# Memory projections of a hybrid encoder layer: whole fp32 matmuls in place of split fp32r ones, with earlier loads and a new order

## The chip, the cores and the metric

The kernel runs on one core of one Trainium2 chip. The metric is the device time of one launch in microseconds, taken over several runs; the time before is the median of three. The profile is of one further execution.

## The reference, cut to what matters

One layer of a streaming encoder over 1024 tokens of width 1024, in fp32:

```
h = rms_norm(x);  p = h @ w_in                      # 31 column tiles of 128 in the kernel
y = concat(rwkv7(p_a), conformer_conv(p_b), hgrn2(p_c), stick_breaking(p_d))
x = x + y @ w_out
h = rms_norm(x);  m = rms_norm(mem)                 # mem: 256 rows
q = h @ wq;  k = m @ wk;  v = m @ wv                # 4 heads of 256
o = softmax(q k^T / 16) v;  x = x + o @ wo;  out = rms_norm(x)
```

The four mixers are independent of each other until `w_out`. The memory `mem` depends on nothing before it. The kernel folds the products of weights with the memory: `keys = wq k^T` and `vals = v wo` for each head, so that the second sub-layer is `softmax(h @ keys) @ vals`.

## The kernel before, in words

**Split numbers.** TensorE takes fp32 in two ways here: an fp32 matmul, or an fp32r matmul on rounded numbers. For most products the kernel writes an operand as a rounded high part and a remainder and issues three fp32r matmuls (high by high, low by high, high by low). Weights are split by POOL (`whi` at line 855, `wlo` at line 856), activations by ACT (high) and DVE (low). The small products inside the mixers are fp32 matmuls of 64 by 64 (line 957, 1082, 1094 to 1097) and the block sums with 512 columns (979, 1110 to 1118).

**Stages.** (1) `xn`, `xT`: rows of x are normed and transposed into `act_hi`, `act_lo`. (2) The input projection, 31 tiles of `w_in`; each is 16 pieces (8 of k for each half of the tokens) of three matmuls with 512 columns (lines 911 to 913). (3) The mixers: a recurrent chain (`lora` to `rfin`, twice, then `hgate` to `hfin`, twice), a convolution chain on DVE, and a stick-breaking chain (`sbz`, `sbt`, `sbv`, 12 units for each pair of heads). In a unit, TensorE makes scores (1170) and, after ACT and DVE (a scan at line 1824), transposes (1183) and multiplies by v (1198); a unit waits for the unit before it. (4) The memory tiles: `mk` and `mv` (8 each, 8 pieces of three 256-column matmuls, lines 911 to 913), `qa` (8, 935 to 937, 256 columns, 8 pieces) and `vo` (8, 944 to 946, 512 columns, 4 pieces). `qa` and `vo` results go through six SBUF slots to DRAM (`keys_dram`, `vals_dram`, line 792). (5) `ysplit` (mixer output into `act_hi` by ACT at 1479, `act_lo` by DVE), then 12 "wide" products of 8 row tiles each, 24 matmuls with 256 columns per row tile (1222 to 1224): four with `w_out`, four with keys, four with values; POOL splits their weights too (842, 843).

**Order.** Stages 2 to 4 are interleaved. A planner in Python (`mixer_order`) simulates TensorE, ACT and DVE with fixed costs and picks at each step a chain's head or the next piece of a tile; its result is one list, and each engine's program follows that list in order. `TILE_RANK` orders the tiles, `URGENT` weighs delay of the four chains, `IDLE` weighs idle TensorE, `HOLD` delays two entries, `SUPPLY` is the time that a tile's weights take. Piece costs of the planner are 0.35 us for `mk`, `mv`, `qa` and 0.7 us for the others.

**Buffers and waits.** `mem_hi` to `v_lo`, `mem_raw` and `moved` lie where `act_hi` and `act_lo` lie, so the memory rows are loaded only after the last `w_in` tile (`load_mem`), and `mn` waits for them. Raw weights have two slots (`wraw`), and two more (`moved[2:4]`) for memory tiles. `x2`, `vhi`, `vlo0` lie over the mixers' buffer `A`, `vraw` at the end of `B` (the stick chain's). SP issues all loads and stores in one queue: after the last memory tile it stores, loads `w_out` parts into `vraw` once the stick chain's last output is read, and x into `x2` once all mixers are done. `ysplit` waits for all mixers and all stores.

Of the kernel before, what the change touches and what calls it, by code (L numbers as in the profile page):

```python
# [14 lines left out]
P = 128  # L15
# [14 lines left out]
KK_SCALE = 2.0 ** 16  # L30

# [9 lines left out]
for _n, _k in (("mu", 6), ("mux", 1), ("w0", 2), ("a0", 2), ("k_k", 2), ("k_a", 2), ("r_k", 2), ("rln_g", 2),  # L41
# [18 lines left out]
TILE_RANK = {t: n for n, t in enumerate((  # L60
# [6 lines left out]
HOLD = {('sv', 1): ('minit', 0, 1),  # L67
        ('s', 1, 'v'): ('sbt', 0, 1, 6)}
# [13 lines left out]
def sb_diagonal(th, u):  # L82

    tb, k0, w = sb_units(th)[u]
    return k0 + w == (tb + 1) * P

# [125 lines left out]
def mixer_order():  # L212
# [31 lines left out]
    for i in range(2):  # L244
# [4 lines left out]
    mem = [(("mn", 0), [("AE", 1.7), ("D", 1.3)], all_in), (("mn", 1), [("AE", 1.7), ("D", 1.3)], []),  # L249
           (("mT", 0), [("P", 0.9), ("A", 1.2), ("D", 1.4)], [("mn", 0)]),  # L250
           (("mT", 1), [("P", 0.9), ("A", 1.2), ("D", 1.4)], [("mn", 1)])]
    for n in range(KT):
        want("mk", n, after=[("mT", 1)])
    for n in range(KT):
        want("mv", n, after=[("mT", 1)])
    for n in range(KT):
        want("qa", n, after=[("proj", "mk", KT - 1, 0)])
# [36 lines left out]
    def read_out(kind, h):  # L294

        g, what = kind[0], kind[-1]
        if what == "gate" or (g, what) == ("h", "q"):
            return [("AS", 0.6), ("D", 0.7)]
        if (g, what) == ("cv", "glu"):
            return [("AS", 0.6)]  # L300
        if g in ("rw", "xw"):
            return [("A", 0.6)] + [("D", 1.9)] * h
        if (g, what) == ("cv", "val"):
            return [("D", 0.7)]
        if g in ("mk", "mv"):
            return [("A", 0.4), ("D", 0.45)]
        return [("A", 0.6)]
# [4 lines left out]
    while any(chains) or tiles or pieces:  # L312
# [16 lines left out]
        if pieces:  # L329
# [3 lines left out]
            if k == h == 0:  # L333
                done["weights"] = max(supplied, tile_over[-2]) + SUPPLY
                waits.append("weights")
            cost = [("P", 0.35 if kind[0] in ("mk", "mv", "qa") else 0.7)]
# [87 lines left out]
def program(nc, x, mem, w_in, w_out, wq, wk, wv, wo, lora, chan, norms, fconst, mconst, out, keys_dram, vals_dram):  # L424
    with ExitStack() as ctx:
# [7 lines left out]
        mem_hi, mem_lo, k_hi, k_lo, v_hi, v_lo = (sb(f"mem{n}", [P, KT, M], F32R) for n in range(6))  # L433
        mem_raw = sb("mem_raw", [P, 2, D])
        moved = sb("moved", [P, 4, HALF])
# [36 lines left out]
        with ExitStack() as st:  # L472
            _below = st.enter_context(nc.sbuf_tensor("below", [P, T], F32))
# [5 lines left out]
            vraw = st.enter_context(nc.sbuf_tensor("vraw", [P, 2, 2, 256], F32))  # L479
# [81 lines left out]
        raw_slots, raw_last, raw_plan = [wraw[:, 0], wraw[:, 1], moved[:, 2, :], moved[:, 3, :]], {}, []  # L561
        for t in tiles_of(SCHED):
            for q in range(2):
                m = len(raw_plan)
                if t[0] in ("mk", "mv", "qa", "vo"):
                    slot = min(range(4), key=lambda s: raw_last.get(s, (-1, 0))[0])
                else:
                    slot = min(range(2), key=lambda s: raw_last.get(s, (-1, 0))[0])
# [6 lines left out]
        tile_no = {tuple(t): n for n, t in enumerate(tiles)}  # L575
        shifted = [t for t in tiles if t[0] == "xw" or (t[0] == "rw" and t[2] in "rkv")]
        shift_no = {tuple(t): n for n, t in enumerate(shifted)}
        for name, *a in SCHED:
            a = tuple(a)
            if name in ("xT", "mT", "hT"):  # L580
                for q in range(2):
                    pj.plan((name,) + a + (q,), reads=2)
            elif name == "piece":
                if a[-1] == 0:
                    both = a[-3] == "gate" or a[0] in ("mk", "mv") or (a[0], a[-3]) == ("h", "q")
# [83 lines left out]
        def mixers_done(eng):  # L669
# [7 lines left out]
        moves = [("qa", n, h) for n in range(KT) for h in range(2)]  # L677
        moves += [("vo", hd, nh, h) for hd in range(4) for nh in range(2) for h in range(2)]
        move_slots = [moved[:, 0, :], moved[:, 1, :]] + [mem_raw[:, i, h * HALF:(h + 1) * HALF]
                                                         for i in range(2) for h in range(2)]  # L680

        def moved_slot(j):
            return move_slots[j % len(move_slots)]

# [31 lines left out]

        hx, hb, hVt, hKt = 1, 2, 7, 8
# [5 lines left out]
        def _(sp):  # L723
# [6 lines left out]
            def load_w(n):  # L730
                kind = tiles[n]
                src, c = weight_columns(kind) if kind[0] != "vo" else ("wo", 0)
                for q in range(2):
                    slot, before, _ = raw_plan[2 * n + q]
                    if before is not None:
                        sp.wait_ge(sem("w_split"), before + 1)
                    elif slot >= 2:
                        sp.wait_ge(sem("m_scaled"), 2)
# [20 lines left out]
            loaded_mem = False  # L759
            def load_wides(first, last):  # L760
                for m in range(first, last):
                    src = {"o": w_out, "s": keys_dram, "f": vals_dram}[wides[m][0]]
                    if wides[m] == ("s", 0):
                        wait_stored(sp, len(moves))
                    c = wides[m][1] * 256
                    for q in range(4):
                        u = 4 * m + q
                        if u >= 2:
                            sp.wait_ge(sem("v_split"), u - 1)
                        else:  # L770
                            so.wait_read(sp, ("o", 1, 1))
                        sp.dma_start(vraw[:, u % 2], src[2 * P * q:2 * P * (q + 1), c:c + 256].rearrange(
                            "(k p) n -> p k n", p=P)).then_inc(sem(f"v_loaded{u % 2}"), 16)

            def load_mem():

                for i in range(2):
                    sp.dma_start(mem_raw[:, i, :], mem[i * P:(i + 1) * P, :]).then_inc(sem("mem_loaded"), 16)
                sp.dma_start(moved[:, 0:2, :].rearrange("p a n -> p (a n)"),
                             norms[NORM_MEM:NORM_MEM + 1, :].broadcast_to([P, D])).then_inc(sem("mem_loaded"), 16)  # L780

            def store(j):

                kind, stored = moves[j], sem(f"stored{j % len(move_slots)}")
                pj.wait_read(sp, kind)
                if kind[0] == "qa":
                    _, n, h = kind
                    dst = keys_dram[n * P:(n + 1) * P, h * HALF:(h + 1) * HALF]
                else:
                    _, hd, nh, h = kind  # L790
                    dst = vals_dram[(2 * hd + h) * P:(2 * hd + h + 1) * P, nh * HALF:(nh + 1) * HALF]
                sp.dma_start(dst, moved_slot(j)).then_inc(stored, 16)

            first_move = tiles.index(["qa", 0])
            for n in range(1, len(tiles)):
                if tiles[n] == ["mk", 0]:
                    for t in tiles[:n]:
                        pj.rd_open(sp, tuple(t) + (1,))
                    load_mem()
                load_w(n)  # L800
                for j in range(2 * (n - 2 - first_move), 2 * (n - 1 - first_move)):
                    if j >= 0:
                        store(j)
            for j in range(2 * (len(tiles) - 2 - first_move), 2 * (len(tiles) - first_move)):
                store(j)
            load_wides(0, 1)
            mixers_done(sp)
            for i in range(TT):
                sp.dma_start(x2[:, i, :], x[i * P:(i + 1) * P, :]).then_inc(sem(f"x2_loaded{i}"), 16)
# [15 lines left out]
        def _(pool):  # L825
# [4 lines left out]
            def split_wides(first):  # L830
                for m in range(first, len(wides)):
                    for q in range(4):
# [4 lines left out]
                        elif q == 0 and m == 0:  # L837
                            pool.wait_ge(sem("rw_done"), 2)
                        elif q == 0:
# [6 lines left out]
            for n in range(len(tiles)):  # L846
                for q in range(2):
# [3 lines left out]
                    if n >= 2:  # L851
                        used = tuple(tiles[n - 2])
                        pj.rd_open(pool, used + (0 if used[0] in ("mk", "mv") else 1,))
                    hi, lo = whi[:, n % 2, 4 * q:4 * q + 4, :], wlo[:, n % 2, 4 * q:4 * q + 4, :]
# [5 lines left out]
        def _(pe):  # L860
# [22 lines left out]
            def mT(i):  # L883
                pe.wait_ge(sem("m_scaled"), i + 1)
                transposed("mT", mem_raw[:, i, :], i)
# [5 lines left out]
            def piece(*a):  # L891
# [3 lines left out]
                n = tile_no[kind]  # L895
                if kind[0] in ("qa", "vo"):
                    return mem_piece(kind, n, h, k)
                cols = slice(0, M) if kind[0] in ("mk", "mv") else hs(h)
                key = kind + (h,)
                if k == 0:  # L900
                    if n == 0:
                        pj.wait_read(pe, ("xT", 4 * h + 3, 1))
                    if kind == ("mk", 0):
                        pj.wait_read(pe, ("mT", 1, 1))
# [5 lines left out]
                hi, lo = (mem_hi, mem_lo) if kind[0] in ("mk", "mv") else (act_hi, act_lo)  # L910
# [7 lines left out]
            def mem_piece(kind, n, h, k):  # L918

                key = kind + (h,)  # L920
                if k == 0:
                    if h == 0 and kind[0] == "qa":
# [7 lines left out]
                if kind[0] == "qa":  # L930
                    if k == 0:
# [6 lines left out]
                    last = k == 3  # L938
# [985 lines left out]
```

## Time and profile before

| what | value |
|---|---|
| time, median of 3 runs (lowest, highest) | 1221.07 us (1218.0, 1221.88) |
| profiled execution: its time, its span | 1218.03 us, 1216.1 us |
| TensorE busy (matmul), weight load | 1084.1 us (89%), 943.0 us (78%) |
| DVE, ACT, POOL busy | 606.9 us, 386.0 us, 392.9 us |
| mean granted TensorE clock | 0.944 of full |

In the profile, "busy" of TensorE has modelled ends: matmuls overlap, so the sum of durations is above the time in which they start. The distance from one start to the next tells the rate. "PEclk" is the granted clock as a share of 2.4 GHz. An fp32 matmul appears as two MATMUL records, an fp32r one as one.

### The profile page before, as it was taken

The numbers are of one execution on the slowest core, as the hardware profiler recorded it, in microseconds if no ns is written. First come the engines' busy times: TensorE is split into PE (matmuls) and PEld (weight loads), VectorE is DVE, ScalarE is ACT, GpSimd is POOL, SyncE is SP. The second block draws the span as 40 slices with busy tenths as digits, with TensorE's granted clock in tenths as the row PEclk, the third lists the DMA queues.
The fourth block names the chain that finished last, engine by engine and source line by source line (L and its number), as shares of the span: only waits on it lengthen the run. The fifth ranks groups of instructions, "written<-read, shape, count | busy, mean of one in ns | idle before, by whom it ended". The sixth has DMA issues, their size and how long they took to land.

```text
span 1216.1 us, 26370 instructions
## 1 busy us (share of the span) xinstructions
PE 1084.1 (89%) x11376; PEld 943.0 (78%) x11376; DVE 606.9 (50%) x831; ACT 386.0 (32%) x646; POOL 392.9 (32%) x355
## 2 busy tenths in 40 slices
PE   4799998998999979899999879888859989998995
PEld 3578797786687976687877668887649988998995
DVE  5414865689276334433575785543341164455114
ACT  6312301301534113455532553344420062123003
POOL 1324200154133001223312036998745322422220
PEclk8889999899899998899999879998969999999998
DMA  5201100011011000111110123456562111111103
GB/s 182 72 26 44 37 4 3 19 35 52 18 35 36 5 3 9 27 35 36 43 28 2 53 62 88 117 166 206 183 237 73 36 36 36 59 47 36 36 18 139
DMA packets 82994, 72.28 MB, mean 59 GB/s; under 512 B 3968, under 2 KB 72640, under 8 KB 82880
## 3 DMA queue, kind: packets, MB, share of 16 engines
q1 hardware_dynamic: 82880, 70.61, 18.7%
q8 instruction: 90, 1.47, 0.5%
q14 instruction: 24, 0.20, 0.0%
HBM read 58.01 MB, written 12.58 MB: 58 GB/s over the span
## 4 chain that ended last, share of the span: by engine, by line
PE 59%; DVE 19%; ACT 9%; POOL 8%; issue 3%; DMA 2%; DVEq 0%; POOLq 0%; SPq 0%; ACTq 0%
PE bank L957 11%; PE bank L1222 7%; PE bank L1224 7%; PE bank L1223 7%; PE bank L911 6%; PE bank L912 6%; PE bank L913 6%; POOL wlo L856 5%; DVE yT L1519 4%; DVE A L1516 3%; ACT A L1243 3%; POOL whi L855 2%; DVE A L1519 2%; DVE late L1519 1%; PE duo L1170 1%
## 5 line engine op out<-in xcount | busy, mean ns | idle before, releaser
L855 POOL TENSOR_SCALAR whi<-wraw 128x512 fp32r<-128x512 f32 x94 | 78.5, 835 | 497.3 <-PE bank L913 463.3
L1222 PE MATMUL bank<-vhi,act_hi 128*128 128x256 f32 x768 | 220.3, 287 | 18.5 <-POOL vlo L843 14.8
L1223 PE MATMUL bank<-vlo,act_hi 128*128 128x256 f32 x768 | 217.9, 284 | 0.0
L1224 PE MATMUL bank<-vhi,act_lo 128*128 128x256 f32 x768 | 217.8, 284 | 0.0
L911 PE MATMUL bank<-act_hi,whi 128*128 128x512 f32 x496 | 207.6, 419 | 5.1 <-DVE yT L1590 3.5
L912 PE MATMUL bank<-act_lo,whi 128*128 128x512 f32 x496 | 198.2, 400 | 0.0
L913 PE MATMUL bank<-act_hi,wlo 128*128 128x512 f32 x496 | 197.8, 399 | 0.0
L957 PE MATMUL bank<-A 64*64 64x64 f32 x4608 | 153.1, 223 | 18.5 <-DVE A L1673 8.7
L957 PEld LDWEIGHTS bank<-A 64*64 64x64 f32 x4608 | 146.0, 139 | 29.1 <-DVE A L1516 13.8
L1222 PEld LDWEIGHTS bank<-vhi,act_hi 128*128 128x128 f32 x768 | 147.7, 192 | 20.8 <-issue 9.0
L1223 PEld LDWEIGHTS bank<-vlo,act_hi 128*128 128x128 f32 x768 | 148.1, 193 | 0.0
L856 POOL TENSOR_TENSOR wlo<-wraw,whi 128x512 fp32r<-128x512 f32 x94 | 145.0, 1542 | 7.8
L1224 PEld LDWEIGHTS bank<-vhi,act_lo 128*128 128x128 f32 x768 | 147.2, 192 | 0.0
L911 PEld LDWEIGHTS bank<-act_hi,whi 128*128 128x128 f32 x496 | 94.7, 191 | 33.6 <-issue 5.7
L913 PEld LDWEIGHTS bank<-act_hi,wlo 128*128 128x128 f32 x496 | 94.4, 190 | 23.3
L912 PEld LDWEIGHTS bank<-act_lo,whi 128*128 128x128 f32 x496 | 94.8, 191 | 22.4 <-issue 2.2
L842 POOL TENSOR_SCALAR vhi<-vraw 128x512 fp32r<-128x512 f32 x48 | 33.5, 698 | 186.5 <-PE bank L1224 151.8
L1519 DVE SCALAR_TENSOR_TENSOR yT<-yT,chn 128x1023 f32<-128x1023 f32 (+30 forms) x62 | 89.9, 1450 | 2.2
L1846 DVE TENSOR_TENSOR x<-x,bank 128x256 f32<-128x256 f32 x64 | 26.9, 421 | 122.2 <-PE bank L1224 121.7
L1243 ACT ACTIVATE A<-A 128x256 f32<-128x256 f32 (+2 forms) x98 | 61.5, 628 | 71.3 <-DVE A L1516 25.9
L1519 DVE SCALAR_TENSOR_TENSOR B<-duo,B 128x1024 f32<-128x1024 f32 (+3 forms) x24 | 23.0, 958 | 118.2 <-ACT B L1243 118.1
L1516 DVE TENSOR_TENSOR A<-A 128x256 f32<-128x256 f32 (+2 forms) x92 | 68.1, 741 | 14.6 <-ACT A L1243 11.7
(167 smaller groups left out, 1629.5 us busy)
## 6 DMA issues: line engine op xcount, KB each, us to landing
wraw<-in_w_in SPq DMA_DIRECT2D x62, 256.0 KB, 2.9
A<-in_x SPq DMA_DIRECT2D x8, 512.0 KB, 3.7
vraw<-in_w_out SPq DMA_DIRECT2D x16, 256.0 KB, 2.6
x<-in_x SPq DMA_DIRECT2D x8, 512.0 KB, 8.5
vraw<-keys_dram SPq DMA_DIRECT2D x16, 256.0 KB, 2.7
vraw<-vals_dram SPq DMA_DIRECT2D x16, 256.0 KB, 2.7
out<-late SPq DMA_DIRECT2D x8, 512.0 KB, 2.6
keys_dram<-mem_raw SPq DMA_DIRECT2D x10, 256.0 KB, 3.6
```

Of the source, the lines that this page charges most:

```text
L855: done(pool, nc.gpsimd.tensor_scalar(hi, raw_view[slot], 1.0, 1.0, ALU.mult, ALU.mult), "w_hi")
L856: done(pool, nc.gpsimd.tensor_tensor(lo, raw_view[slot], hi.bitcast(F32), ALU.subtract), "w_split")
L911: mm(bank, wh, hi[:, k, cols], start=k == 0, stop=False)
L912: mm(bank, wh, lo[:, k, cols], start=False, stop=False)
L913: ins = mm(bank, wl, hi[:, k, cols], start=False, stop=k == KT - 1)
L957: ins = mm(bank[r, c * CH:(c + 1) * CH], a(r, col), b(r, col), start=n == 0, stop=n == len(terms) - 1)
L1222: mm(bank, ah, vhi[:, (m + 1) % 2, k, :], start=k == 0, stop=False)
L1223: mm(bank, ah, wide_lo(m)[:, k, :], start=False, stop=False)
L1224: ins = mm(bank, al, vhi[:, (m + 1) % 2, k, :], start=False, stop=k == KT - 1)
L1243: return nc.scalar.activation(out, in_, func, **kw)
L1516: ok(V.tensor_tensor(out, a, b, op), name)
L1519: ok(V.scalar_tensor_tensor(out=out, in0=a, scalar=s, in1=b, op0=op0, op1=op1), name)
```

## The change

- `mk`, `mv`, `vo` are computed with fp32 matmuls on whole numbers: a piece is one matmul instead of three. POOL splits no weights for these 24 tiles (`unsplit`); TensorE reads them from the raw slots. The memory's transposes give one fp32 tensor `memT` (ACT alone reads the bank), `mv` gives one fp32 tensor `valsT`, so the DVE part of `mT` and of `mv` goes away. `qa` stays split.
- The freed space makes `moved` 16 slots: ten for raw weights (twelve with `wraw`), six for results.
- Memory rows and their gain go into `A` (rows 11, 12 and 3). They are loaded after the recurrent mixer is done (`rw_done` 2) and the first `hfin` (`h_done` 1), from SP's queue ahead of the weights of tile `mem_at`. `mn` may run before the last `w_in` tile; `mT` waits for all of them.
- x for the residual is loaded into `x2` within the tile loop (`x2_at`), after `h_done` 2 and `m_scaled` 2. `vraw` moves to row 0 of `A`: the first two `w_out` parts are loaded ahead of the last stores, and POOL may split wide 0 once `rw_done` is 2 and `mT` is read.
- Stores lag four tiles (before: two). `qa` and `mv` tiles alternate. The planner's constants, `TILE_RANK` and `HOLD` are new; piece costs are 0.43 us for `mk` and `mv`, 0.35 for `qa`, 0.86 for `vo`.

```diff
-SUPPLY = 3.768
-SWITCH = 0.119
-IDLE = 2.803
-URGENT = (12.926, 0.964, 1.121, 2.909)
-AHEAD = 0.948
-PIECES_TOGETHER = 1
+SUPPLY = 3.764
+UNSPLIT = 1.2
+SWITCH = 0.175
+IDLE = 13.308
+URGENT = (46.84, 3.527, 2.162, 41.323)
+AHEAD = 2.927
+PIECES_TOGETHER = 3
...
-HOLD = {('sv', 1): ('minit', 0, 1),
-        ('s', 1, 'v'): ('sbt', 0, 1, 6)}
+HOLD = {('h', 1, 'gate'): ('sbt', 0, 1, 7)}
...
+def unsplit(kind):
+
+    return kind[0] in ("mk", "mv", "vo")
...
-    mem = [(("mn", 0), [("AE", 1.7), ("D", 1.3)], all_in), (("mn", 1), [("AE", 1.7), ("D", 1.3)], []),
-           (("mT", 0), [("P", 0.9), ("A", 1.2), ("D", 1.4)], [("mn", 0)]),
+    mem = [(("mn", 0), [("AE", 1.7), ("D", 1.3)], [("hfin", 0)]), (("mn", 1), [("AE", 1.7), ("D", 1.3)], []),
+           (("mT", 0), [("P", 0.9), ("A", 1.2)], [("mn", 0)] + all_in),
...
-            cost = [("P", 0.35 if kind[0] in ("mk", "mv", "qa") else 0.7)]
+            cost = [("P", {"mk": 0.43, "mv": 0.43, "qa": 0.35, "vo": 0.86}.get(kind[0], 0.7))]
...
-            _below = st.enter_context(nc.sbuf_tensor("below", [P, T], F32))
+            vraw = st.enter_context(nc.sbuf_tensor("vraw", [P, 2, 2, 256], F32))
             x2 = st.enter_context(nc.sbuf_tensor("x2", [P, TT, D], F32))
...
+        mem_at = min(first_mem, tiles_begun(("hfin", 0)) + 2)
+        x2_at = tiles_begun(("hfin", 1)) + 3
...
             def load_mem():
 
+                sp.wait_ge(sem("rw_done"), 2)
                 for i in range(2):
-                    sp.dma_start(mem_raw[:, i, :], mem[i * P:(i + 1) * P, :]).then_inc(sem("mem_loaded"), 16)
...
+                    sp.dma_start(A[:, MEM_ROWS + i, :], mem[i * P:(i + 1) * P, :]).then_inc(sem("mem_loaded"), 16)
+                sp.wait_ge(sem("h_done"), 1)
...
+            def load_x2(i):
+
+                if i == 0:
+                    sp.wait_ge(sem("h_done"), 2)
+                    sp.wait_ge(sem("m_scaled"), 2)
...
             for n in range(1, len(tiles)):
-                if tiles[n] == ["mk", 0]:
-                    for t in tiles[:n]:
-                        pj.rd_open(sp, tuple(t) + (1,))
+                if n == mem_at:
                     load_mem()
                 load_w(n)
...
+                if 0 <= n - x2_at < TT:
+                    load_x2(n - x2_at)
+                if n - STORE_LAG >= first_move:
+                    store(n - STORE_LAG)
+            early = range(2 if x2_at < len(tiles) else 0)
+            for u in early:
+                load_wide(u)
...
-            for n in range(len(tiles)):
+            for n, kind in enumerate(tiles):
+                if unsplit(kind):
+                    continue
...
-                mm(bank, wh, hi[:, k, cols], start=k == 0, stop=False)
-                mm(bank, wh, lo[:, k, cols], start=False, stop=False)
-                ins = mm(bank, wl, hi[:, k, cols], start=False, stop=k == KT - 1)
...
+                elif kind[0] == "vo":
...
+                    ins = mm(bank, valsT[:, 2 * kind[1] + k, h * P:(h + 1) * P], rows, start=k == 0, stop=k == 1)
+                    last = k == 1
                 else:
...
+                    ins = mm(bank[:, 0:M], raw_view[slot][:, k % 4, :], memT[:, k, :], start=k == 0, stop=k == KT - 1)
```

## Rows read from the trace of the kernel before

**Rows 1.** The chain of waits from 718 to 883 us, its shares by line.
```profile
by line: POOL wlo L856 34.2%; POOL whi L855 16.3%; issue 9.2%; ACT B L1243 6.9%; PE bank L957 5.0%; PE duo L1170 3.0%; PE duo L1183 2.7%; PE bank L911 2.3%; PE bank L944 2.2%; DMA wraw<-in_wq 2.1%; DMA moved<-in_wo 2.0%; DMA moved<-in_wk 2.
```
**Rows 2.** Engines by stretch: length, busy of each (instructions), clock, DMA share, GB/s.
```profile
683.00:723.00 40.00, 26.25 (x489) 23.32 (x487) 35.55 (x64) 19.55 (x43) 4.61 (x6) 0.81 0.23 74
...
842.00:883.00 41.00, 35.42 (x199) 27.59 (x199) 11.64 (x9) 18.47 (x25) 29.85 (x29) 0.89 0.49 168
883.00:904.00 21.00, 6.61 (x26) 5.76 (x27) 13.79 (x8) 8.63 (x9) 14.54 (x8) 0.55 0.53 181
...
683.00:883.00 200.00, 168.42 (x1775) 148.62 (x1773) 110.44 (x148) 88.66 (x145) 136.79 (x128) 0.92 0.42 134
```
**Rows 3.** Groups of instructions, POOL, 718 to 879 us: busy us, mean ns, idle.
```profile
L856 POOL TENSOR_TENSOR wlo<-moved,whi 128x512 fp32r<-128x512 f32 x32 | 44.6, 1394 | 2.7
L855 POOL TENSOR_SCALAR whi<-moved 128x512 fp32r<-128x512 f32 x32 | 24.1, 752 | 75.9 <-DMA moved<-in_wk 64.3 <-PE bank L913 6.5 <-PE bank L946 2.6
```
**Rows 4.** Groups by shape, TensorE, 683 to 883 us.
```profile
L911 PE MATMUL bank<-mem,whi 128*128 128x256 f32 x128 | 39.0, 305 | 5.2 <-POOL wlo L856 5.1
...
L957 PE MATMUL bank<-A 64*64 64x64 f32 x640 | 27.3, 250 | 10.2 <-DVE A L1673 6.0 <-DVE A L1516 4.0
...
L944 PE MATMUL bank<-whi,mem 128*128 128x512 f32 x32 | 14.8, 464 | 7.8 <-POOL wlo L856 7.8
...
L1170 PE MATMUL duo<-B 64*128 64x128 f32 x144 | 11.8, 298 | 0.0
```
**Rows 5.** Instructions in order of time, TensorE, 742 to 744 us (13 starts apart).
```profile
742.34 0.28 PE L912 MATMUL bank<-mem,whi 128*128 128x256 f32 x1
...
743.86 0.28 PE L913 MATMUL bank<-mem,wlo 128*128 128x256 f32 x1
```
**Rows 6.** The same view, 320.9 to 325.3 us; an fp32 matmul is two records.
```profile
320.97 0.39 PE L912 MATMUL bank<-act_lo,whi 128*128 128x512 f32 x1
321.20 0.40 PE L913 MATMUL bank<-act_hi,wlo 128*128 128x512 f32 x1
...
323.68 1.02 PE L1118 MATMUL bank<-yT,fcst 128*128 128x512 f32 x2
324.54 1.02 PE L1117 MATMUL bank<-yT,fcst 128*128 128x512 f32 x2
```
**Rows 7.** The chain of waits in order of time: start, us, what.
```profile
732.02 3.06 PE bank L957 x96
...
803.75 1.11 PE duo L1170 x16
```
**Rows 8.** Groups by shape, TensorE, 480 to 682 us.
```profile
L911 PE MATMUL bank<-act_hi,whi 128*128 128x512 f32 x194 | 80.8, 416 | 3.5 <-DVE yT L1590 3.5
...
L957 PE MATMUL bank<-A 64*64 64x64 f32 x640 | 22.1, 220 | 3.4 <-DVE A L1673 2.7 <-DVE A L1798 0.3
```
**Rows 9.** Groups by shape, DVE, 683 to 883 us.
```profile
L1824 DVE TENSOR_TENSOR_SCAN B<-fcst,B 128x512 f32<-128x512 f32 x12 | 20.2, 1683 | 0.4
```
**Rows 10.** Groups by shape, DVE, 480 to 682 us.
```profile
L1824 DVE TENSOR_TENSOR_SCAN B<-fcst,B 128x512 f32<-128x512 f32 x10 | 12.9, 1288 | 0.4
```
**Rows 11.** Instructions in order of time, DVE: L1519 begins a stick unit.
```profile
716.55 0.42 DVE L1519 SCALAR_TENSOR_TENSOR B<-duo,B 128x256 f32<-128x256 f32 x1 [1.62 <-ACT B L1243]
...
749.25 1.22 DVE L1516 TENSOR_TENSOR yT<-yT,A 128x1024 f32<-128x1024 f32 x1
...
784.92 1.22 DVE L1519 SCALAR_TENSOR_TENSOR B<-duo,B 128x1024 f32<-128x1024 f32 x1 [3.55 <-ACT B L1243]
...
798.37 0.69 DVE L1519 SCALAR_TENSOR_TENSOR B<-duo,B 128x512 f32<-128x512 f32 x1 [2.37 <-ACT B L1243]
...
808.29 1.22 DVE L1519 SCALAR_TENSOR_TENSOR B<-duo,B 128x1024 f32<-128x1024 f32 x1 [5.16 <-ACT B L1243]
```
**Rows 12.** Instructions in order of time, DVE, behind the mixers' end.
```profile
904.10 0.42 DVE L1846 TENSOR_TENSOR x<-x,bank 128x256 f32<-128x256 f32 x1 [2.96 <-PE bank L1224]
```
**Rows 13.** Instructions in order of time, ACT, behind the mixers' end.
```profile
885.96 8.58 ACT L1479 CAST act_hi<-yT 128x1024 fp32r<-128x1024 f32 x8 [2.69 <-DMA vals_dram<-moved]
```

More of the change, by code:

```diff
@@ L254, in mixer_order @@
     for n in range(KT):
+        want("qa", n, after=[("proj", "mk", KT - 1, 0)])
         want("mv", n, after=[("mT", 1)])
-    for n in range(KT):
-        want("qa", n, after=[("proj", "mk", KT - 1, 0)])
     for hd in range(4):
@@ L559, in program @@
         SCHED = schedule()
-        raw_slots, raw_last, raw_plan = [wraw[:, 0], wraw[:, 1], moved[:, 2, :], moved[:, 3, :]], {}, []
+        raw_users = []
+        raw_slots, raw_last, raw_plan = [wraw[:, 0], wraw[:, 1]] + [moved[:, n, :] for n in range(6, 16)], {}, []
         for t in tiles_of(SCHED):
@@ L564, in program @@
                 m = len(raw_plan)
+                raw_users.append((tuple(t), sum(not unsplit(u) for u, _ in raw_users)))
                 if t[0] in ("mk", "mv", "qa", "vo"):
-                    slot = min(range(4), key=lambda s: raw_last.get(s, (-1, 0))[0])
+                    slot = min(range(len(raw_slots)), key=lambda s: raw_last.get(s, (-1, 0))[0])
                 else:
@@ L674, in mixers_done, with split_tiles, wait_used @@
             so.wait_read(eng, ("o", 1, 1))
[L677 to L680, printed above, removed]
+        moves = [tuple(t) + (h,) for t in tiles if t[0] in ("qa", "vo") for h in range(2)]
+        move_slots = [moved[:, i, :] for i in range(6)]
         def moved_slot(j):
             return move_slots[j % len(move_slots)]
+        def split_tiles(n):
+            return sum(not unsplit(t) for t in tiles[:n])
+        def wait_used(eng, kind):
+            pj.rd_open(eng, kind + (0 if kind[0] in ("mk", "mv") else 1,))
         def wait_stored(eng, count):
@@ L734, in load_w @@
                     slot, before, _ = raw_plan[2 * n + q]
[L735 to L736 removed]
+                    if before is not None and unsplit(raw_users[before][0]):
+                        wait_used(sp, raw_users[before][0])
+                    elif before is not None:
+                        sp.wait_ge(sem("w_split"), raw_users[before][1] + 1)
                     elif slot >= 2:
[L738 removed]
+                        for t in tiles[first_mem - 2:first_mem]:
+                            pj.rd_open(sp, tuple(t) + (1,))
                     if kind[0] == "vo":
@@ new lines, in store @@
+            def store(n):
+                kind = tuple(tiles[n])
+                if kind[0] not in ("qa", "vo"):
+                    return
+                for h in range(2):
+                    j = moves.index(kind + (h,))
+                    pj.wait_read(sp, kind + (h,))
+                    if kind[0] == "qa":
+                        dst = keys_dram[kind[1] * P:(kind[1] + 1) * P, h * HALF:(h + 1) * HALF]
+                    else:
+                        _, hd, nh = kind
+                        dst = vals_dram[(2 * hd + h) * P:(2 * hd + h + 1) * P, nh * HALF:(nh + 1) * HALF]
+                    sp.dma_start(dst, moved_slot(j)).then_inc(sem(f"stored{j % len(move_slots)}"), 16)
@@ L806, in _ @@
[L806 to L809, printed above, removed]
+                if 0 <= n - x2_at < TT:
[5 more added lines that the diff above has]
+                load_wide(u)
+            for n in range(len(tiles) - STORE_LAG, len(tiles)):
+                store(n)
@@ L810, in _ @@
+            for i in range(max(0, len(tiles) - x2_at), TT):
+                load_x2(i)
+            for u in range(len(early), 2):
+                load_wide(u)
+            load_wide(2)
+            load_wide(3)
             for n, t in enumerate(tiles[-2:]):
```

130 lines of the change are left out of this document (59 added, 71 removed), and 12 rows, old and new, of the table TILE_RANK.

## The prediction

> **What bounds the kernel now.** I read four views: the slices of the page (where TensorE is not full or its clock is low), the engines by stretch, the chain of waits, and the groups by shape for the counts. TensorE is the engine to watch, at 89% of the span, but the share hides where it is short. The slices show it short at the start, in the recurrent chains, and from 683 us, where the last `w_in` tile ends, to 904 us, where the wide products are under way. The change is about that stretch.
>
> It has three pieces. From 683 to 723 us TensorE has 26.3 busy us of 40 at a mean clock of 0.81 [rows 2]: no `w_in` tile is left, the memory rows are not normed, and only the recurrent chain runs, for which DVE is 35.6 us busy. From 718 to 883 us the chain of waits lies for half its length on POOL's splits, 34.2% and 16.3% [rows 1]: POOL is busy 136.8 us in 683 to 883 with 128 instructions [rows 2], 64 pairs of 1.39 and 0.75 us [rows 3], 4.3 us a tile with 32 tiles. From 883 to 904 us TensorE is busy 6.6 us at a mean clock of 0.55 [rows 2], waiting for `ysplit` and the split of the first wide weights.
>
> **How full TensorE really is.** Its busy time has modelled ends, so I count instructions and multiply by the distance between starts. fp32r with 256 columns: 13 starts in 1.52 us, 0.117 us each [rows 5]. fp32r with 512: 0.23 us [rows 6]. fp32 with 512: a pair of records every 0.86 us [rows 6]. 64 by 64 records: 0.0325 us (96 in 3.06) [rows 7]; lines 1170 and 1198: about 0.065 us (16 in 1.11, the first one's length in it) [rows 7]. Work from 683 to 883 us: memory tiles 3 x 128 + 3 x 64 matmuls with 256 columns and 3 x 32 with 512 (one line of each three stands in [rows 4], the `qa` lines are like the 911 one with x64) = 67.1 + 22.3 = 89.4 us; 64 by 64 records 640 and 64 more, 22.9; lines 1170 and 1198, 144 records each, 18.4 [rows 4]; transposes and small ones, of 0.11 us at most but for four block sums, 12.3. Sum 143.0 of 200 us: TensorE is 57 us short of full. By the same count the stretch from 480 to 682 us, where chains and `w_in` tiles are mixed and POOL is not in the way, has 194 x 3 x 0.232 = 135.0, (640 + 192) x 0.0325 = 27.0, and 21.1 of other chain work, 183.1 of 202 us: 9.4% short [rows 8].
>
> **The memory tiles in fp32.** A piece with 256 columns goes from 3 x 0.117 = 0.35 us to one fp32 matmul. The trace has none with 256 columns and 128 rows; half of the 512-column one is 0.43 us. Bounds: 0.35 (equal to now) and 0.86 (no gain from half the columns, which the 256 to 512 step of fp32r, 0.117 to 0.23, speaks against). I take 0.43: 128 pieces x 0.08 = +10 us. `vo`: 32 pieces from 0.70 to 0.86 = +5 us. TensorE gains 15.5 us of work, 143.0 to 158.5 us. POOL loses 24 x 4.3 = 103 us. What is left for it, 8 `qa` tiles, alternates with `mv` tiles: 4.3 us of POOL beside 2.8 + 3.4 us of TensorE, so it is covered even if POOL were a third slower; without the cover each `qa` tile would cost 1.5 us, 12 in all. DVE loses four transposes' low parts of 0.69 us and eight `mv` steps of 0.42 us; they wait for nobody, so I count nothing.
>
> **How long the stretch becomes.** From below: all work without a gap, 158.5 us, so -41.5. From above: the 57 us stay, 215.5, so +15.5. I take the idle share of the 480 to 682 us stretch, the nearest with the same mixture and no POOL bound: 158.5 / 0.906 = 175 us, that is 25 us less. The 40 us before 723 take part, because `mn` no longer waits for the last `w_in` tile and `mk` weights need no split: TensorE gets `mk` pieces under DVE's recurrent work. What is late next is the stick chain. Its second pair has 12 units, each after the one before. A full unit took 13.4 us, one of half width 9.9 [rows 11], so 6.4 us plus 7.0 us per 512 columns; 12 x 6.4 + 9 x 7.0 = 140 us. Its first DVE step is at 716.6 us now [rows 11], so it can't end before 857; my 883 - 25 = 858 is at that end. The two bounds nearly meet, and for this reason I don't take more than 25.
>
> The chain's scans are a place where this may give more. The scan of 512 columns takes 1.68 us in this stretch [rows 9] and 1.29 us from 480 to 682 us [rows 10], where POOL splits less; without the splits the chain could be 12 x 0.4 and some 3.6 us for the narrower ones shorter, 8 us, and end at 849 us. That is a rival below. The Trainium skill (SBUF — State Buffer, section on the two separate sides) says that GpSimd and VectorE take their shared port pair as an exclusive lock when VectorE has two SBUF inputs, as this scan has; by that rule, which the trace agrees with, the 8 us would be gained.
>
> **Loads and SP's queue.** The tiles' loads (32 x 0.52 MB), the stores (8.4 MB) and x (4.2 MB) come into the 175 us, 29.4 MB or 168 GB/s. From 842 to 883 us the core moved 168 GB/s at a DMA share of 0.49 [rows 2], so I count nothing; `vo` tiles in a row would want 1.05 MB in 3.4 us, 305 GB/s, and at most could cost a third of their 27 us, 9 us, if the rate stopped at 210. In SP's queue load and store alternate with a lead of four tiles, some 13 us against loads that take 3. Moved in that queue: memory rows and gain (three issues) ahead of a `w_in` tile, eight x loads and two `vraw` loads ahead of `vo` stores; each issue is below 1 us with slots already full. The waits that go with them are a rival below.
>
> **Behind the mixers.** Today the last store is seen by ACT at 885.96 [rows 13], and the first row tile of wide 0 is added at 904.10 [rows 12], since its four weight parts are loaded only when the stick chain has ended and are then split, 3.7 us each. With the first parts loaded and split before, only `ysplit` is left: ACT 1.07 us (8 in 8.58) [rows 13], then a DVE step of 1.2 to 1.7, so a start some 2.7 us behind ACT's, at 888.7 on the old scale, 24 matmuls at the lower clock level (the 0.55 of [rows 2]) x 0.23 = 5.6, end 894.3. That is 10 us less. Bounds: 0, if the parts come late after all, and 15, if the clock stays up.
>
> **The order of the stages up to 683 us.** Of 683 us TensorE lacks 105 by the same count, 34 of them in the first 50 us, which the change doesn't touch. The new weights of the planner can move the other 71 either way. No row says in which; I take 0, with -15 and +15, a fifth of it, as bounds.
>
> **Sum.** 1218.0 - 25 - 10 = 1183 for the profiled execution. The median of the runs shown is 3 us (0.25%) above that execution, so I forecast 1186 us as the median.
>
> **Rivals.**
> *Only the waits that the profile records go away.* TensorE's recorded waits for POOL in memory pieces are 5.1 us at line 911, 7.8 at 944 [rows 4], and 3.3 at 935: 16.2 us. The stretch is then 200 + 15.5 - 16.2 = 199, and with the 10 us behind it 1210. For it: DVE and ACT chains also bound the first 40 us. Against it: the chain of waits is half POOL.
> *The stick chain is the bound, and its scans quicken without POOL.* The mixers end 8 us earlier than in the sum: 1178. For it: the two durations of the scan. Against it: TensorE has 158.5 us of work in the stretch and then would have to be full for all but 7 us.
> *The new order also fills the mixers.* Another 20 us of the 71 go: 1165. For it: three pieces together and heavier weight on idle time; against it: chains there wait for DVE, and more pieces don't shorten them.
> *The early loads stay late.* If SP stands at `h_done` 2 behind a late recurrent end, x and the first wide parts come as before: 1195. Against it: today `hfin(1)` is done at 750 us [rows 11], 130 us before the last tile.
> *Slower: the stick chain comes later and ends last.* The weight of that chain falls against the idle weight (1.12 to 2.80 becomes 2.16 to 13.3). Its second pair takes 140 us from its start. If its first DVE step comes at 776 instead of 716.6, the mixers end at 776 + 140 = 916, 33 us later than now, less 10 behind them: 1244. It decides from a step some 40 us later than today's. Against it: the first pair has room (only ten of its full scans lie in the 202 us of [rows 10], where 140 us would hold the whole pair); and memory tiles can't start before its second pair's `w_in` tiles, which wait for the first.
>
> **How the numbers follow.** Forecast 0.36 (1180 to 1196), recorded waits only 0.18, quicker scans 0.10, fuller mixers 0.15, early loads late 0.08, cases near no change (1215 to 1227, parts of the two costs above) 0.05, slower 0.08. A change under 0.3% can't be told from none here. Faster 0.87, same 0.05, slower 0.08. The range runs from 1163 to 1214: it holds the first five cases but their tails.
>
> **What would show it.** Right: POOL busy near 290 us; two MATMUL records 0.43 us apart in all for a memory piece; memory work from the first microseconds behind the last `w_in` tile; from that tile to the first added wide row some 185 us where it is 221; the chain of waits there on ACT, DVE and TensorE; the first wide row added within 10 us of `ysplit`'s start. Wrong: an fp32 piece well above 0.43 us, TensorE waiting for raw weights in `vo`, or a last `w_in` tile later than 700 us.

## The result, and the profile after

The changed kernel takes 1223.80 us (median of 20 runs, 1220.89 to 1226.59), the kernel before 1218.94 us (20 runs, 1216.27 to 1223.50): ratio 1.0038, 95% interval 1.0027 to 1.0049. It is slower by 0.4%; the forecast was 1186.

I divide both profiled executions at the start of the last `w_in` piece and the last start of a memory matmul. Work of TensorE is counted as in the prediction (records times distance of starts); idle is the rest.

| us | before | after | difference |
|---|---|---|---|
| last `w_in` matmul | 681.5 | 740.6 | +59.1 |
| of that work, idle | 576.0, 105.5 | 590.8, 149.8 | +14.8, +44.3 |
| from there to the last memory matmul | 200.7 | 154.6 | -46.1 |
| of that work, idle | 144.4, 56.3 | 144.5, 10.1 | +0.1, -46.2 |
| from there to the end of the span | 333.9 | 325.5 | -8.4 |
| span | 1216.1 | 1220.7 | +4.6 |

The idle time of TensorE wasn't removed but moved: 46 us less behind the last `w_in` tile, 44 us more ahead of it. What is left is 15 us more work (the fp32 pieces) against 8 us gained behind the mixers.

The changed kernel by stretches (us from the start, length, busy us and instructions of PE, PEld, DVE, ACT, POOL, granted clock, DMA share, GB/s), beside [rows 2]:

```profile
476.00:741.40 265.40, 220.10 (x2368) 179.61 (x2368) 144.74 (x210) 111.47 (x165) 34.31 (x32) 0.91 0.08 21
741.40:896.00 154.60, 151.64 (x1173) 120.50 (x1172) 62.57 (x77) 73.07 (x110) 38.67 (x36) 1.00 0.62 192
580.00:680.00 100.00, 64.76 (x1032) 56.29 (x1031) 67.47 (x99) 46.47 (x70) 7.46 (x7) 0.83 0.06 17
760.00:780.00 20.00, 20.00 (x127) 17.36 (x128) 9.96 (x15) 7.30 (x12) 0.45 (x1) 1.00 0.94 290
```

The second row is the stretch that the change is about: TensorE busy 151.6 of 154.6 us at full clock, POOL 38.7 us where it had 136.8. The third is new: 100 us in the middle of the mixers with TensorE busy 64.8 us at a clock of 0.83. No engine is full there. The kernel before, in the same 100 us:

```profile
580.00:680.00 100.00, 96.62 (x1127) 77.05 (x1126) 58.38 (x91) 42.41 (x63) 20.85 (x16) 1.00 0.07 19
```

What is missing there is `w_in` work. Before, TensorE starts 88 `w_in` pieces in these 100 us, after 18: none begins between 588.9 and 676.7 us, where before no such pause behind 482 us is longer than 5.4 us. That pause holds the loss:

```profile
588.90:676.70 87.80, 52.56 (x981) 46.46 (x979) 60.18 (x91) 39.85 (x63) 3.77 (x4) 0.81 0.07 20
```

By the same count TensorE has 40 us of work in these 87.8 us and is idle for 48.

What TensorE waited for from 476 to 741 us (us in total, times, longest):

```profile
PE duo L1225 <- DVE B L1558: 20.6, 4, 7.7
PE bank L999 <- DVE A L1714: 9.3, 14, 1.3
PE bank L999 <- DVE A L1558: 7.3, 2, 4.8
```

before, from 476 to 681 us, the same wait (there lines 1183 and 1516):

```profile
PE duo L1183 <- DVE B L1516: 2.3, 1, 2.3
```

and after from 741 to 896 us, where POOL's part is 0.5 us:

```profile
PE duo L1225 <- DVE B L1558: 1.2, 2, 0.8
PE bank L983 <- ACT mem L1325: 1.0, 1, 1.0
PE bank L975 <- POOL wlo L897: 0.5, 1, 0.5
```

Line 1225 transposes a stick unit's weights, line 1558 is DVE's step before it. Where a `w_in` piece stands in the list between the two, this wait is hidden; where none is left in the list at that place, TensorE stands.

When the stick chain runs is read from the first and last start of its DVE step (24 units; before is line 1519, after 1561):

```profile
L1519 DVE SCALAR_TENSOR_TENSOR B<-duo,B x24: 424/1091/1226, 317.0 to 868.6; 128x1024 f32<-128x1024 f32 x12, 128x256 f32<-128x256 f32 x4, 128x512 f32<-128x512 f32 x4, 128x768 f32<-128x768 f32 x4
```
```profile
L1561 DVE SCALAR_TENSOR_TENSOR B<-duo,B x24: 424/1092/1226, 478.1 to 880.5; 128x1024 f32<-128x1024 f32 x12, 128x256 f32<-128x256 f32 x4, 128x512 f32<-128x512 f32 x4, 128x768 f32<-128x768 f32 x4
```

The last unit comes only 12 us later, the first 161 us later. Four `w_in` tiles are left at 588.9 us, and none may begin yet: in the planner's code the second pair's three tiles, the last of all, wait for the first pair's output for the second half of the tokens (written at 611.1 us before, at 687.1 after), and `HOLD` ties the gate tile of hgrn to the first pair's last unit, whose DVE step starts at 666.0. The gate tile begins at 676.7 us, the other three at 690.1, 706.6 and 727.1.

### The profile page after: what moved, and what is told of

Read it like the earlier page. It is cut to its first block, busy times and chain, and to the rows that moved or that the text cites. A ratio compares the mean times of both kernels' runs of the same rounds, so it can differ in the third digit from the quotient of the medians.

```text
span 1220.7 us, 25877 instructions
## 1 busy us (share of the span) xinstructions
PE 1092.0 (89%) x11216; PEld 940.0 (77%) x11216; DVE 591.1 (48%) x819; ACT 375.7 (31%) x638; POOL 291.0 (24%) x259
## 4 chain that ended last, share of the span: by engine, by line
PE 65%; DVE 20%; ACT 9%; issue 2%; DMA 1%; SPq 1%; POOL 0%; DVEq 0%; ACTq 0%; POOLq 0%
PE bank L999 11%; PE bank L948 7%; PE bank L949 6%; PE bank L1264 6%; PE bank L950 6%; PE bank L1266 6%; PE bank L1265 6%; DVE yT L1561 5%; DVE A L1558 3%; ACT A L1285 2%; PE bank L983 2%; PE bank L988 2%; ACT B L1285 2%; DVE B L1865 1%; DVE late L1561 1%
## 5 line engine op out<-in xcount | busy, mean ns | idle before, releaser
L896 POOL TENSOR_SCALAR whi<-wraw 128x512 fp32r<-128x512 f32 x62 | 56.7, 915 | 548.4 <-PE bank L950 445.6
L897 POOL TENSOR_TENSOR wlo<-wraw,whi 128x512 fp32r<-128x512 f32 x62 | 98.9, 1596 | 5.2
```

The lines of the kernel that those rows point to most:

```text
L896: done(pool, nc.gpsimd.tensor_scalar(hi, raw_view[slot], 1.0, 1.0, ALU.mult, ALU.mult), "w_hi")
L897: done(pool, nc.gpsimd.tensor_tensor(lo, raw_view[slot], hi.bitcast(F32), ALU.subtract), "w_split")
```

## The experiments

Each ratio is to the kernel before, run on the same chip, with its 95% interval. An edit of the order is an edit of the planner and its constants; in the first two runs it takes the places of the memory's norm and tiles in the list with it.

### Parts and order apart

```
# old_order_new_parts: the changed kernel with
# the planner's constants, ranks, costs and memory tiles of before;
# the memory rows are loaded early, but normed behind the last w_in tile
-URGENT = (46.84, 3.527, 2.162, 41.323)
-HOLD = {('h', 1, 'gate'): ('sbt', 0, 1, 7)}
+URGENT = (12.926, 0.964, 1.121, 2.909)
+HOLD = {('sv', 1): ('minit', 0, 1), ('s', 1, 'v'): ('sbt', 0, 1, 6)}
...
# new_order_old_parts: the kernel before with those of the changed one;
# its memory pieces keep their places in the list, in the order mk, mv, qa, vo,
# and the memory rows are normed behind the last w_in tile
+    s += old_memory_order(mixer_order())
```

> The new kernel's parts (fp32 memory tiles without splits, early loads) under the old kernel's order word for word (its planner and constants, mv tiles ahead of qa tiles, memory rows normed behind the last w_in tile). Theory A, the new order costs some 58 us up to the last w_in tile and the parts by themselves gain: last w_in tile near 683 us as before, the stretch from there to the end of the memory tiles 165 to 180 us, 8 to 10 us less behind the mixers, 1175 to 1190 us in all. Rival B, the parts gain only because the new order has moved chain work ahead of the memory tiles: the stretch stays near 190 to 200 us, 1200 to 1215 us in all.

> The old kernel's parts (split memory tiles, late loads) under the new kernel's order; only the memory tiles among themselves stand in the old sequence, since the old stores need it, and the memory rows are normed behind the last w_in tile. Theory A: last w_in tile near 741 us, then a memory stretch bound by POOL's splits at 4.2 us a tile, 170 to 190 us, and the old 21 us behind it: 1245 to 1270 us. Rival C, the late last w_in tile has to do with the new parts (memory loads in SP's queue) and not with the order: last w_in tile near 683 to 700 us and 1200 to 1225 us.

Measured: 1198.47 us, ratio 0.9837 (0.9822 to 0.9851), and 1254.84 us, ratio 1.0305 (1.0288 to 1.0323). The parts, without the early norm, are worth -20 us, the order alone costs +37. The second run is as theory A has it. The first lies between the ranges of theory A (1175 to 1190, stretch 165 to 180 us) and rival B (1200 to 1215, stretch 190 to 200): its last `w_in` matmul came as A said, its stretch was longer. TensorE's idle time ahead of the last `w_in` matmul follows the order alone: 105.5 us before and 105.2 with the old order and new parts; 149.8 after and 150.1 with the new order and old parts. So the loss is in the list, and no early load or fp32 piece takes part in it.

In the old order with new parts the stretch is 187 us, where the prediction had 175. Two windows of it show where:

```profile
681.50:719.50 38.00, 25.85 (x498) 22.42 (x496) 34.72 (x61) 20.35 (x44) 0.00 (x0) 0.87 0.32 85
719.50:868.80 149.30, 146.52 (x1126) 116.23 (x1126) 63.20 (x76) 68.64 (x101) 37.87 (x36) 1.00 0.57 178
```

From 719.5 us TensorE is full; in the first 38 us it has the busy share and the low clock of [rows 2] as if nothing had changed: the rows are loaded at 627 us, but this list norms them only from 711 us on and has no memory piece until then.

### The loads, the rows and the splits of the change

```
# late_loads: x and the first w_out parts as before
-            early = range(2 if x2_at < len(tiles) else 0)
-                if 0 <= n - x2_at < TT:
-                    load_x2(n - x2_at)
+            mixers_done(sp)
...
# late_rows: memory rows only after all w_in tiles
+        mem_at = first_mem
+    mixers[at:at] = [("mn", 0), ("mn", 1)]      # mn directly ahead of mT
...
# idle_splits: POOL splits all 32 memory tiles, mk, mv, vo don't read the parts but wait for them
+                        pe.wait_ge(sem("w_split"), 2 * t + k + 1)
...
```

> The new kernel with the residual rows and the four parts of the first w_out block loaded only when all mixers are done, as in the old kernel. Theory A: 8 to 12 us slower than the new kernel (1228 to 1236 us), the first wide row added some 18 us behind ysplit's start in place of 7 to 8. Rival: within 3 us of it, if the DMA queues had carried them in time anyway; or faster by some us, if the early x loads slow the memory tiles' loads (290 GB/s and a DMA share of 0.94 at 760 to 780 us).

> The new kernel with the memory rows loaded and normed only behind the last w_in tile, as in the old kernel; all else is new. The new order with old parts had its first memory matmul 25 us behind the last w_in tile, the new kernel has it 12.8 us behind. Theory A (POOL's splits give 10.6 us of the 24 us by which the new parts shorten the stretch, early rows most of the rest): first memory matmul 20 to 26 us behind the last w_in tile, 8 to 13 us slower than the new kernel, 1231 to 1237 us. Rival: TensorE's chain work fills the wait, within 3 us of 1224.

> The new kernel, in which POOL again splits the weights of all 32 memory tiles and TensorE waits for each split, though the 24 mk, mv and vo tiles still take the whole numbers: the split's result is not used there. Order, fp32 matmuls and early loads are the new ones. Theory A, POOL's splits bound the old memory stretch: from the last w_in tile (740.6 us) to the last memory matmul 170 to 185 us where the new kernel has 154.6, 1240 to 1255 us in all, and the 512-column scans of the stick chain back from 1.35 to 1.6 us. Rival, the stretch is shorter only by the order and the fp32 matmuls (one instruction where three stood): within 5 us of 1224.

| | time, us | ratio (interval) | stretch, us | behind it, us |
|---|---|---|---|---|
| after | 1223.80 | 1.0038 (1.0027 to 1.0049) | 154.6 | 325.5 |
| late_loads | 1232.49 | 1.0109 (1.0092 to 1.0126) | 154.7 | 335.6 |
| late_rows | 1235.09 | 1.0138 (1.0107 to 1.0169) | 166.1 | 325.4 |
| idle_splits | 1235.44 | 1.0141 (1.0111 to 1.0170) | 165.2 | 329.2 |

Each part has its worth where the prediction put it, behind the stretch or in it: 9 us for the loads, 11 for the rows, 12 for the splits. idle_splits is far outside its rival's 5 us, but stayed below what theory A asked (1240 to 1255 us, stretch 170 to 185), so the splits are worth less than expected in this list. The 12 are not only the wait. POOL in idle_splits and in the changed kernel, both from 740 us to the mixers' end:

```profile
L895 POOL TENSOR_TENSOR wlo<-moved,whi 128x512 fp32r<-128x512 f32 x54 | 72.9, 1351 | 4.5
L895 POOL TENSOR_TENSOR wlo<-wraw,whi 128x512 fp32r<-128x512 f32 x10 | 15.6, 1563 | 0.8
```
```profile
L897 POOL TENSOR_TENSOR wlo<-moved,whi 128x512 fp32r<-128x512 f32 x16 | 22.4, 1402 | 1.3
```

DVE's scan of 512 columns, first in idle_splits, then in the changed kernel:

```profile
L1867 DVE TENSOR_TENSOR_SCAN B<-fcst,B 128x512 f32<-128x512 f32 x12 | 19.9, 1659 | 0.4
```
```profile
L1865 DVE TENSOR_TENSOR_SCAN B<-fcst,B 128x512 f32<-128x512 f32 x12 | 16.2, 1348 | 0.4
```

With 64 pairs of splits the scan takes 1.66 us, with 16 pairs 1.35, by the same DVE instructions on the same operands. The Trainium skill (SBUF — State Buffer, section on the two separate sides) says that a VectorE instruction with two SBUF inputs and a GpSimd instruction that reads SBUF take a shared port pair as an exclusive lock. The trace agrees in the direction, 1.66 us against 1.35; it doesn't show the lock itself.

### The stick chain moved alone

```
# old_late_stick: the kernel before; searched_late_stick: the same line in searched_order (below)
+        ('sbz', 0, 0, 0): ('rfin', 1),      # first stick unit after the end of the second rwkv pair
```

> The old kernel with one more HOLD entry: the stick chain's first unit waits for the end of the second recurrent pair (rfin 1), as it stands in the new order (first unit at 476 us there, 314 us in the old kernel). Theory A, the late start of the stick chain is what the new order costs: the second pair's w_in tiles can't come before the first pair's end, so the last w_in tile moves from 681 to some 735 us and the whole goes to 1240 to 1260 us (the planner counts +33). Rival D, the cost lies in the sequence of gate and h tiles, not in the stick chain: below 1228 us.

> The faster order of the search with the same one HOLD entry (first stick unit behind rfin 1). Theory A: most of its gain goes, 1215 to 1235 us (the planner counts +53 us), last w_in tile 740 to 755 us where it was 689. Rival D: below 1195 us.

Measured: 1261.41 us, ratio 1.0357 (1.0325 to 1.0388), 44 us above the kernel before; and 1228.47 us, ratio 1.0084 (1.0062 to 1.0106), 51 above its own base. The second is in theory A's range, the first 1 us above it, with the last `w_in` matmul at 747 us where some 735 was expected; rival D fails in both. One held entry takes the kernel before to the picture of the changed one: first stick score at 471.9 us, last `w_in` matmul at 747.1, idle 156.3 us ahead of it, and TensorE's largest wait from 476 to 747 us is the same:

```profile
PE duo L1184 <- DVE B L1517: 20.7, 4, 10.7
PE bank L958 <- DVE A L1674: 8.5, 14, 1.3
```

No `w_in` piece begins there from 621.1 to 692.0 us. A late stick chain is thus enough for such a loss. Whether its undoing is enough for the gain is another question:

```
# early_stick: the changed kernel with
-    ... ('s', 0, 'q'), ('h', 0, 'q'), ('s', 0, 'k'), ('h', 1, 'f')))}
+    ('s', 0, 'k'), ('rw', 0, 'k'), ('rw', 1, 'r'), ...
# early_stick_even: and
-URGENT = (46.84, 3.527, 2.162, 41.323)
+URGENT = (46.84, 3.5, 2.16, 3.5)
```

> The changed kernel with one edit to TILE_RANK: ('s', 0, 'k') first instead of last but one; constants, HOLD and all parts stay. The planner's own clock for it: first stick unit 281 (411 in the changed kernel), last w_in tile 610 (673), but the second hgrn's last step 831 (692) and the whole list 914 (829). Theory A (the late stick chain is the cost of the new list, and an early one gives it back by itself): first stick unit near 330 us on the chip, last w_in tile some 60 us earlier, the stretch back to some 175, time 1185 to 1200 us. Theory B (a list is one whole: in this one the recurrent chain is pressed behind the stick chain when that starts early, and the planner's end is the better guide): the last w_in tile is earlier as under A, near 680, but hgrn ends late and the mixers end after 950, time 1280 to 1320 us. In both the first stick unit is early; what tells them apart is the end.

> As early_stick, and URGENT (46.84, 3.5, 2.16, 3.5) instead of (46.84, 3.527, 2.162, 41.323): the weight of the memory's chain is no longer nearly that of the recurrent one. The planner's clock: first stick unit 281, last w_in tile 611, last hgrn step 724, whole list 852 (829 in the changed kernel, 799 before, 779 in the searched order). Theory A (an early stick chain is enough): 1185 to 1200 us. Theory B (the planner's end, with the same offset as for the changed kernel): 1223.8 + 24 = 1248, from 1235 to 1262 us.

Measured: 1326.95 us, ratio 1.0894 (1.0863 to 1.0924), and 1257.30 us, ratio 1.0320 (1.0295 to 1.0345). Theory A fails in both. Theory B's range holds for early_stick_even (1235 to 1262 us); early_stick came out 7 us above its 1280 to 1320. In early_stick the first unit comes at 348.8 us and the last `w_in` matmul at 684.7, as early as before; but a heavy weight of the memory's chain puts the memory tiles next, and they run out at 853 us, while 120 of the stick chain's 288 score records are still to come:

```profile
685.00:853.00 168.00, 141.08 (x1044) 113.14 (x1043) 38.39 (x63) 56.24 (x96) 30.28 (x32) 0.89 0.49 151
853.00:1004.00 151.00, 75.19 (x969) 63.05 (x967) 77.68 (x109) 53.41 (x75) 10.96 (x11) 0.66 0.14 50
```
```profile
PE duo L1225 <- DVE B L1558: 49.4, 9, 8.3
```

The wait for line 1558 is the same one, 49.4 us now, behind the last tile. Tiles are the filler for the chains' waits, and this list used them up 148 us before its chains were done (853.0, and the last stick output at 1000.0 to 1000.7). In early_stick_even, with the light weight, the last memory matmul comes at 926.8 us and the stick chain ends earlier, but 1088 of the 64 by 64 records stand behind the last `w_in` matmul, where the changed kernel has 256, and the stretch is 239 us.

### Other lists with the changed kernel's parts

```
# searched_order
-IDLE = 13.308;  URGENT = (46.84, 3.527, 2.162, 41.323);  AHEAD = 2.927;  PIECES_TOGETHER = 3
+IDLE = 19691536.179;  URGENT = (12652978.549, 0.0, 0.0, 0.0);  AHEAD = 4.981;  PIECES_TOGETHER = 1
...      # another TILE_RANK, HOLD = {}
# searched_order2, searched_order3: found with SUPPLY = 4.15, SWITCH = 0.175
```

> The new kernel with other planner constants and no HOLD entries, found by a search that lets the kernel's own planner count its end: it gives 780 us where the new order has 829 and the old planner in the old kernel 799. Theory A, order alone is what costs: the planner's last w_in tile moves from 673 to 623 us, so the chip's from 741 to some 691, and the whole goes from 1224 to 1170 to 1185 us. Rival, the planner's counts don't carry over to the chip at this size: above 1205 us.

> The new kernel's parts with an order from a longer search in which the planner's weights take 4.15 us (what a tile's two split pairs take on the chip) and a switch of matmul kind 0.175 us; the planner's last w_in tile is at 604 us and its end at 798 (under these costs it gives the first searched order 938). If the planner's costs are near the chip: 1160 to 1180 us. If not: above 1185 us.

> As the last, from another start of the search: the planner's last w_in tile at 596 us, its end at 802. 1163 to 1183 us under the same theory, above 1188 us if the planner's costs are off.

| | time, us | ratio (interval) | first stick score | last `w_in` | idle to it | stretch (idle) |
|---|---|---|---|---|---|---|
| searched_order | 1177.29 | 0.9660 (0.9634 to 0.9686) | 283.6 | 688.7 | 98.1 | 159.9 (15.5) |
| searched_order2 | 1217.55 | 0.9997 (0.9982 to 1.0012) | 304.7 | 698.4 | 122.2 | 191.4 (32.3) |
| searched_order3 | 1205.33 | 0.9887 (0.9859 to 0.9916) | 204.6 | 676.2 | 102.0 | 201.1 (40.0) |

searched_order beats both kernels, by 3.4% and 3.8%. It is the tightest comparison with the changed kernel: the same parts, the same TensorE work to the last `w_in` matmul (590.6 and 590.8 us) and from there to the last memory matmul (144.4 and 144.5), and 51.7 us less idle ahead of it for 5.4 us more behind. Its row from 476 to 689 us, to be read beside the first row of the changed kernel:

```profile
476.00:689.00 213.00, 197.55 (x2064) 158.56 (x2063) 123.01 (x177) 102.13 (x145) 42.95 (x36) 0.97 0.10 29
```

The other two are misses: both expected less than 1184 us if the planner's costs were near the chip's, and both came out where the expectation put costs that are off. They start the stick chain early as well and yet leave hgrn's 64 by 64 work (22.9 and 25.0 us against 8.4), and its waits, in the last stretch.

One number comes near to telling the times of all lists: the end that the planner itself counts. With the new parts, time less that end is 398, 420 and 404 us for the three searched lists (ends 778.9, 797.8, 801.4), 400 for the old order (798.8), 395 for the changed kernel (828.6), 404 for early_stick_even (853.1), 413 for early_stick (914.1). It doesn't order them strictly: searched_order2 and the old order have ends 1 us apart and times 19 us apart. And the ends of searched_order2 and 3 are counted with `SUPPLY` 4.15, the others with 3.76 to 3.77.

## Why the prediction was wrong

**The order of the stages up to 683 us.** This is the step that failed: "No row says in which; I take 0, with -15 and +15, a fifth of it, as bounds." It was +59.1 us to the last `w_in` matmul, which came at 740.6, where the prediction itself names a time after 700 as a sign of being wrong. 14.8 of it are chain work done earlier and given back behind; 44.3 are idle time, three times the bound, and the pause without a `w_in` piece from 588.9 to 676.7 us holds 48 us of idle time. The bound took for granted that a new list moves idle time of the old size, 71 us; a list decides how long chains run with nothing to fill their waits, and for that 71 us is no limit.

**The rival that held.** "The stick chain comes later and ends last" (0.08) had the mechanism, and I argued it away with the wrong pair: the first pair had 140 us of units in 202 us, but it was the first pair that came late, from 317 to 478 us. The second pair's first DVE step came at 755.63, 39 us later than in [rows 11], at the rival's point of decision, and its last, the output, at 891.44 (0.69 us long); 136.5 us, close to the 140 worked out. The rival's price of 1244 was for a step at 776. With the measured start its own sum is 1218.0 + (755.6 + 140 - 883) - 10 = 1220.6, where the profiled execution took 1222.43. That the sum comes out so near is in part luck: TensorE was nearly full in the stretch too, and its last memory matmul (895.2) is behind the chain's last output.

**How long the stretch becomes.** -25 predicted, -46.1 measured. By the runs it is two terms. With the old order the parts without the early norm gave -13.5 (200.7 to 187.2), since the memory pieces stood behind hgrn's work in the list; the claim that TensorE gets `mk` pieces in the 40 us before 723 failed there. The new order gave -22.3 alone (178.4), because 14.6 us of 64 by 64 work had gone ahead, and then the parts another -23.8: 10.6 by splits, 11.5 by rows. The 154.6 measured lie below the prediction's lower bound of 158.5, all work without a gap, because that bound took the chain work in the stretch as fixed: 144.5 us of work were left there.

**The memory tiles in fp32.** Held. A record of a 256-column piece is 0.215 us ((1.67 - 0.38) / 6), two of them 0.43; a 512-column record 0.43 ((3.60 - 0.59) / 7):

```profile
756.49 1.67 PE L988 MATMUL bank<-mem,moved 128*128 128x256 f32 x7
...
883.25 3.60 PE L983 MATMUL bank<-wraw,mem 128*128 128x512 f32 x8
```

Together 128 x (0.43 - 0.351) + 32 x (0.86 - 0.696) = +15.3 us, where 15.5 stood. POOL is busy 291.0 us; near 290 was expected.

**Scans.** The rival's mechanism is real (1.68 to 1.35 us), but the chain of second-pair units was 136.5 us and TensorE's work, not it, set the stretch.

**Loads and SP's queue.** Held: eight x loads and the weights of `mk`, `qa` and `mv` tiles share 760 to 780 us at 290 GB/s and a DMA share of 0.94, and TensorE is busy all 20 us. Single x issues held SP's queue for up to 2.74 us, where below 1 us stood; TensorE didn't wait for it.

**Behind the mixers.** -10 predicted, -8.4 measured, and in late_loads this part is 10.1 us longer than in the changed kernel. ACT begins `ysplit` at 899.26, TensorE 2.4 us later:

```profile
899.26 8.59 ACT L1521 CAST act_hi<-yT 128x1024 fp32r<-128x1024 f32 x8 [2.75 <-DMA vals_dram<-moved]
900.41 14.10 DVE L1558 TENSOR_TENSOR act_lo<-yT,act_hi 128x1024 fp32r<-128x1024 f32 x8 [8.28 <-ACT act_hi L1521]
901.69 0.58 PE L1264 MATMUL bank<-vhi,act_hi 128*128 128x256 f32 x1 [5.88 <-DVE act_lo L1558]
914.54 1.33 DVE L1887 TENSOR_TENSOR x<-x,bank 128x256 f32<-128x256 f32 x3
```

The first row tile is added 15.3 us behind ACT's start, not within 10: in DVE's queue the additions stand behind all eight of its `ysplit` steps. TensorE went on, so this cost little.

**What stays open.** No single entry of the changed list was shown to cause its 44 us; the `HOLD` entry of the gate tile, which is free only at the end of the pause, was not taken out alone. A held stick chain makes such a loss in two other lists, and an earlier one in this list only moves it behind the tiles.

## What to carry to other kernels

A list planned for several engines is a part of the change like any other: price it first, by when each chain starts and how much filler work is left for each chain's waits, and where such a list carries its own planned end, compare those ends; here seven lists kept the same distance to it within 25 us, over times 150 us apart, so such an end can be trusted to some 25 us here. A zero "because no row says" needs a bound as wide as the chain that could move. And a resource that is freed pays only where the list has work to put there.

## What the runs showed of the hardware

DVE's scan of 512 columns took 1.35 us beside 16 pairs of POOL splits and 1.66 beside 64. Single scans beside no POOL instruction took 1.22 to 1.29 us, the longest beside splits 2.34 in idle_splits and 2.40 in the kernel before. Two scans in a row, first in idle_splits beside splits, then in the changed kernel beside none:

```profile
873.50 3.82 DVE L1867 TENSOR_TENSOR_SCAN B<-fcst,B 128x512 f32<-128x512 f32 x2
```
```profile
867.39 2.48 DVE L1865 TENSOR_TENSOR_SCAN B<-fcst,B 128x512 f32<-128x512 f32 x2
```

At a DMA share of 0.94 (290 GB/s) TensorE lost nothing that can be seen in 20 us. In 853 to 1004 us of early_stick, with TensorE busy half of the time, the mean granted clock was 0.66, and a 64 by 64 matmul took 261 ns where it took 220 at full clock:

```profile
L999 PE MATMUL bank<-A 64*64 64x64 f32 x576 | 26.0, 261 | 11.9 <-DVE A L1714 6.7 <-DVE A L1558 2.7 <-DVE A L1839 1.7
```
```profile
L999 PE MATMUL bank<-A 64*64 64x64 f32 x192 | 6.3, 220 | 0.0
```
